# High and low halves in the sparse scores, and an order changed at four places of a two-block network kernel

## The chip, the core and the metric

The kernel runs on one core of a Trainium2 chip. The metric is the device time of one execution in microseconds (us), as the median of several runs. The core's engines work side by side and wait for each other by semaphores: TensorE (PE: matmuls into PSUM), VectorE (DVE), ScalarE (ACT), GpSimd (POOL) and SyncE (SP), which here issues DMAs. Each engine runs its own instructions strictly in order. Inputs, outputs and the state-space tables lie in HBM; everything between is in SBUF.

## The reference, cut to what matters

256 tokens of width 1024 pass two blocks of two layers each, in float32.

```python
# block 1: layer 0 short convolution, layer 1 dilated attention with partial rotary
h = h + mixer(rmsnorm(h)); h = h + relu(rmsnorm(h) @ up)**2 @ down          # mlp
h = h + sigmoid(rmsnorm(h) @ w_gate) * (p @ w_proj)                          # ple
# block 2, layer 0: h += ffn0; h += s5(rmsnorm(h)); h += ffn1; shared keys and values
# s5: per group of 16 channels 64 complex states, x_t = A x_{t-1} + B u_t, y = Re(C x)
y = gelu(y + d_skip * u); h = h + y * sigmoid(y @ w_glu)
# block 2, layer 1: h += ffn2; h += nsa(rmsnorm(h)); h += ffn3
qg = u @ w_qg                      # 16 heads of 64, and 48 gate columns
q = rmsnorm(qg[..., :1024]); gates = sigmoid(qg[..., 1024:])
o = gates[0] * o_cmp + gates[1] * o_selected + gates[2] * o_window
h = h + o @ w_o
# each branch: softmax(q @ k * scale + bias) @ v; 15 compressed keys, 256 selected, 256 window keys
```

## The kernel before, in words

All dense weights are one array of 280 units of 1 MB, 128 partitions by 2048 columns. They stream through a ring of three slots (`RING` = 3). For a unit SyncE loads `raw`, ScalarE copies it to `w_hi` (L1152, a rounded copy of it), VectorE subtracts `w_lo` (`split`, L1952), and TensorE multiplies. Activations are held transposed, channels on partitions, as `x_hi` and `x_lo` too, made in four pairs of chunks (`x_high` on ScalarE, `x_low` on VectorE). A slot comes free when TensorE is done with its unit, and only then can its next high half be written. A product in full accuracy is three matmuls (`exact`, L460 to L462):

```python
nc.tensor.matmul(out, a_hi, b_hi, start=start, stop=False, skip_group_check=True)
nc.tensor.matmul(out, a_hi, b_lo, start=False, stop=False, skip_group_check=True)
return nc.tensor.matmul(out, a_lo, b_hi, start=False, stop=stop, skip_group_check=True)
```

`double_unit` (L507, L509) does the same with two matmuls, of 512 and 256 columns. `zero` products (L481, L904) add zeros, and `keep_warm` issues them so that TensorE has work in a wait.

**Norms.** The scale of a norm isn't applied to the activations. ScalarE squares them (L1176), GpSimd adds the squares (`add_squares`, L1701), TensorE sums over partitions and later broadcasts (`norm_sum`, `norm_bcast`), VectorE and GpSimd make the inverse root, ScalarE copies it to `rs`. The stage is multiplied afterwards.

**Start and convolution.** VectorE begins with a chain of 31 operations on 128x32 (`link`, L2202 to L2221), from which ScalarE makes a sine and a cosine (L1363 and after). Then come low halves and the first splits. The convolution is four triples of units (`conv_triple` on each engine), then the residual stage `sc_out`, then `mlp0`, whose first norm is number `R_SC`. GpSimd does its norm R_IN, then `input_matrices`, which waits for the 31 operations and the sine and cosine, then `four_tables(0, R_SC)`:

```python
make_table(c)
if not c:
    norm(r)
make_table(c + 1)
```

A table is 1.8 MB, stored to HBM and loaded again in the state-space stage. ScalarE's squares are double-buffered, so its third square of a norm waits for GpSimd's first add of that norm (`sq_used`).

**Angles.** The rotary angles are eight small VectorE operations (`angles`, L2163 to L2182), one pair after each of the four gate steps of `ple0`.

**State-space stage.** After `ffn0`, `u5` = h x gain x norm scale is made in eight chunks, and VectorE, ScalarE and GpSimd move it to the layout of groups (`u2`). TensorE does eight `states` (each 24 products, L923) and eight `outputs` (L935, 16 products) and turns the result back (`turn_y`). Between the two VectorE turns the drive (L2405) and scans, GpSimd turns back. The gate unit `glu` follows.

**Sparse attention.** TensorE's queries are four units (`qg`), the gates 48 products of 48 columns between the first and the second unit. Per head `n_scores` multiplies query and keys in plain float32 (two products of 128 queries for the selected and window keys, one for 15 compressed keys per 128 queries). Softmax, transposes (`n_turn`) and values follow, three steps behind each other in a loop over heads. `out_part` multiplies two heads' output into the first two units of `w_o`; the third unit (L460) comes behind the loop, and behind it the fourth (`up_unit(g + 3, ...)`).

## Time and profile before

| | |
|---|---|
| median of 3 runs | 1919.35 us (1918.03 to 1920.93) |
| the profiled execution | 1921.98 us, its span 1920.1 us |
| granted TensorE clock, mean | 0.987 of full speed |
| chain that ended last | PE 84%, DVE 9%, ACT 4%, issue 2%, POOL 1% |
| L1952, weight splits on DVE | x277, 653.4 us, 2361 ns each |
| L1152, high halves of weights on ACT | x280, 534.1 us, 1909 ns each |
| HBM | 318.54 MB read, 174 GB/s over the span |

Times are microseconds from the start of the span; engines overlap, so busy shares don't add up. The chain that ended last is followed back from the last instruction. A line such as L460 is shared by all products that `exact` issues.

### The profile page before, as it was taken

Reading aid. Unit: us, or ns where it says so; the run is one execution under the profiler, and the core shown is the slowest. Engines: PE = TensorE matmul, PEld = TensorE weight load, DVE = VectorE, ACT = ScalarE, POOL = GpSimd, SP = SyncE. Lnnn points to the kernel's source line nnn. Section 1 sums busy time; section 2 is a strip of 40 time slices with the busy share of each in tenths; the row PEclk is TensorE's granted clock in tenths of the full one; section 3 lists DMA queues with packets and bytes.
Section 4 is the critical chain, followed back from the end, with each engine's and each line's share of the span. In section 5 each row is a group of like instructions: output and inputs, shape, how many; then the busy total and the mean of one; then the engine's idle time right before and its main releaser. Section 6 shows DMA issues by size and latency. Waiting matters only on the chain.

```text
span 1920.1 us, 31815 instructions
## 1 busy us (share of the span) xinstructions
PE 1860.1 (97%) x13410; PEld 1716.7 (89%) x13427; DVE 1284.7 (67%) x1503; ACT 927.2 (48%) x1214; POOL 635.5 (33%) x756
## 2 busy tenths in 40 slices
PE   8999999899999999999999989999999999999999
PEld 6979999899999899988997878998989989778998
DVE  6878666666664777677666756666656665657665
ACT  4354445444334554455444245444654454755443
POOL 6968880476753887010001620000000002420000
PEclk9999999999999999999999899999999998999999
DMA  6555564454444566557556315665355642015553
GB/s 243 187 186 214 214 215 181 151 187 165 155 165 144 172 216 215 209 194 289 193 181 214 116 73 205 220 219 182 137 169 193 211 179 88 23 39 181 189 184 110
DMA packets 54954, 336.35 MB, mean 175 GB/s; under 512 B 7915, under 2 KB 13084, under 8 KB 17948
## 3 DMA queue, kind: packets, MB, share of 16 engines
q1 hardware_dynamic: 45648, 297.51, 43.1%
q10 hardware_dynamic: 5068, 22.13, 3.0%
q0 software_dynamic: 4096, 14.68, 2.2%
q8 instruction: 106, 1.74, 0.4%
q14 instruction: 36, 0.29, 0.0%
HBM read 318.54 MB, written 15.75 MB: 174 GB/s over the span
## 4 chain that ended last, share of the span: by engine, by line
PE 84%; DVE 9%; ACT 4%; issue 2%; POOL 1%; ACTq 0%; DVEq 0%; POOLq 0%
PE psum L507 22%; PE psum L460 13%; PE psum L461 13%; PE psum L462 13%; PE psum L509 11%; DVE w_lo L1952 3%; ACT w_hi L1152 2%; DVE both L1959 1%; ACT both L1152 1%; PE psum L935 1%; PE psum L973 1%; PE psum L1093 1%; PE psum L1062 1%; DVE h L1965 1%; PE psum L923 1%
## 5 line engine op out<-in xcount | busy, mean ns | idle before, releaser
L1952 DVE TENSOR_TENSOR w_lo<-raw,w_hi 128x2048 fp32r<-128x2048 f32 x277 | 653.4, 2361 | 200.9 <-ACT w_hi L1152 198.1
L507 PE MATMUL psum<-both,w_hi 128*128 128x512 f32 x1984 | 702.7, 397 | 9.6 <-DVE both L1959 6.8
L1152 ACT ACTIVATE w_hi<-raw 128x2048 fp32r<-128x2048 f32 x280 | 534.1, 1909 | 179.7 <-PE psum L462 178.2
L509 PE MATMUL psum<-both,w_lo 128*128 128x256 f32 x1984 | 556.6, 281 | 0.0
L460 PE MATMUL psum<-both,w_hi 128*128 128x256 f32 x1600 | 464.2, 290 | 16.4 <-DVE both L1959 10.0
L507 PEld LDWEIGHTS psum<-both,w_hi 128*128 128x128 f32 x1984 | 372.7, 188 | 98.0 <-DVE both L1959 7.9
L461 PE MATMUL psum<-both,w_hi 128*128 128x256 f32 x1600 | 454.9, 284 | 0.0
L462 PE MATMUL psum<-both,w_lo 128*128 128x256 f32 x1600 | 454.8, 284 | 0.0
L509 PEld LDWEIGHTS psum<-both,w_lo 128*128 128x128 f32 x1984 | 375.5, 189 | 0.1
L460 PEld LDWEIGHTS psum<-both,w_hi 128*128 128x128 f32 x1600 | 308.6, 193 | 17.1 <-DVE both L1959 11.6
L461 PEld LDWEIGHTS psum<-both,w_hi 128*128 128x128 f32 x1600 | 308.8, 193 | 0.8 <-issue 0.2
L462 PEld LDWEIGHTS psum<-both,w_lo 128*128 128x128 f32 x1600 | 308.7, 193 | 0.0
L1701 POOL TENSOR_TENSOR ssum<-sq 128x512 f32<-128x512 f32 x11 | 18.5, 1683 | 735.9 <-ACT sq L1176 735.9
L1152 ACT ACTIVATE sq<-psum 128x512 f32<-128x512 f32 x120 | 71.7, 598 | 335.7 <-PE psum L509 334.6
L460 PE MATMUL psum<-hid_hi,w_hi 128*128 128x256 f32 x640 | 179.5, 280 | 0.3
L461 PE MATMUL psum<-hid_lo,w_hi 128*128 128x256 f32 x640 | 177.7, 278 | 0.0
L462 PE MATMUL psum<-hid_hi,w_lo 128*128 128x256 f32 x640 | 177.6, 277 | 0.0
L2048 DVE TENSOR_TENSOR ta<-psum,sq 128x512 f32<-128x512 f32 x76 | 52.3, 688 | 106.6 <-ACT sq L1152 106.4
L460 PEld LDWEIGHTS psum<-hid_hi,w_hi 128*128 128x128 f32 x640 | 120.2, 188 | 3.2 <-issue 1.6
L462 PEld LDWEIGHTS psum<-hid_hi,w_lo 128*128 128x128 f32 x640 | 120.8, 189 | 0.0
L461 PEld LDWEIGHTS psum<-hid_lo,w_hi 128*128 128x128 f32 x640 | 120.2, 188 | 0.1
L2099 DVE TENSOR_TENSOR tc<-psum,sq 128x512 f32<-128x512 f32 x44 | 30.4, 692 | 64.3 <-ACT sq L1152 64.3
(402 smaller groups left out, 2504.4 us busy)
## 6 DMA issues: line engine op xcount, KB each, us to landing
raw<-in_weights SPq DMA_DIRECT2D x280, 1024.0 KB, 4.8
table<-tables ACTq DMA_DIRECT2D x8, 1792.0 KB, 8.5
tables<-st POOLq DMA_DIRECT2D x16, 512.0 KB, 4.3
tables<-st POOLq DMA_DIRECT2D x8, 256.0 KB, 5.8
tables<-turns POOLq DMA_DIRECT2D x8, 256.0 KB, 4.4
w<-in_cmp_w ACTq DMA_DIRECT2D x4, 512.0 KB, 5.2
tbl<-in_cmp_w ACTq DMA_DIRECT2D x4, 512.0 KB, 5.2
tbl<-bias_v SPq DMA_DIRECT2D x128, 16.0 KB, 4.7
```

What stands on the lines that cost most here:

```text
L460: nc.tensor.matmul(out, a_hi, b_hi, start=start, stop=False, skip_group_check=True)
L461: nc.tensor.matmul(out, a_hi, b_lo, start=False, stop=False, skip_group_check=True)
L462: return nc.tensor.matmul(out, a_lo, b_hi, start=False, stop=stop, skip_group_check=True)
L507: nc.tensor.matmul(bank, wh[:, cols], both[x][:, c].rearrange("p e t -> p (e t)"), start=c == 0, stop=False, skip_group_check=True)
L509: return nc.tensor.matmul(bank[:, 0:SEQ], wl[:, cols], x_hi[x][:, c], start=False, stop=c == KC - 1, skip_group_check=True)
L923: last = nc.tensor.matmul(SB_[c % 4][:, at:at + SK], w_[:, jj, ri], u2[:, jj, c, :], start=True, stop=True, skip_group_check=True)
L935: last = nc.tensor.matmul(y_of(c, jj), x5[c % 2][:, ri, jj, 0:SK], q_[:, jj, ri], start=False, stop=ri == 1, skip_group_check=True)
L973: last = nc.tensor.matmul(DB[half][0:2 * NCMP, 0:P], blk[rows, l, :, :].rearrange("p c n -> p (c n)"), [w1, w1v][kind][rows, l, :], start= ...
L1152: copy = lambda out, in_, **kw: nc.scalar.activation(out, in_, ACT.Copy, **kw)
L1952: tt(w_lo[:, g % RING], raw[:, g % RING], w_hi[:, g % RING].bitcast(F32), ALU.subtract).then_inc(sem["lo_ready"], 1)
L2048: tt(ta[:], hi_part(pair), low[into], ALU.add).then_inc(sem["a_sum"], 1)
L2099: tt(tc[:], hi_part(B_PAIR), low[1], ALU.add).then_inc(sem["b_sum"], 1)
```

## The change

- Start: VectorE's 31 operations go behind the first (13 of them) and the second triple (18) of the convolution, ScalarE's sine and cosine behind its second. ScalarE's squares R_IN come between its copies of the first weights. SyncE issues the load of the constants behind the second weight unit. GpSimd's code is the same.
- Angles: the third and fourth pair are issued behind the last low half of `ple0`.
- State space: gains are applied without the norm's scale ahead of the norm; the scale is multiplied into `u2`, chunk by chunk, afterwards, from a copy of 32-token rows that ScalarE makes. `states` waits for one chunk's multiply. 14 and 5 + 5 zero products are added, 24 and others taken out. One weight split moves from the end of `ffn0` to behind the scans. The order of the norm's parts changes.
- Sparse attention: gates are 24 products with 48 weight columns and 256 moving ones, copied, transposed and then put through the sigmoid. Scores are three products each of halves; ScalarE and VectorE make the halves of the keys and the queries. The compressed keys are padded to 16 columns.
- The third unit of `w_o` moves piecewise into the end of the loop over heads (`third_rows`).

The diff, cut to its core and moved to the left:

```diff
@@ -274,7 +274,10 @@
-    q2 = sb("q2", [P, NQ, SEQ], scope=t)
+    ks_hi = sb("ks_hi", [P, 2, 2, SEQ], F32R, scope=t)
+    ks_lo = sb("ks_lo", [P, 2, 2, SEQ], F32R, scope=t)
...
@@ -418,7 +422,9 @@
     sp.dma_start(raw[:, u], A["weights"][u]).then_inc(raw_landed[u], 16)
     if u == 0:
         sp.wait_ge(sem["h_landed"], 16 * PAIRS)
+    if u == 1:
         sp.dma_start(con[:], A["con"]).then_inc(sem["con_landed"], 16)
+        sp.wait_ge(raw_landed[1], 16)
...
@@ -903,18 +909,16 @@
 keep_warm(20, XB)
 norm_sum(R_FFN0)
+clear_sums()
+keep_warm(4, XB)
+norm_bcast(R_FFN0)
 keep_warm(6, XB)
-norm_bcast(R_FFN0)
-keep_warm(24, XB)
-clear_sums()
 def states(c):
...
-    for name in ("u2_dve", "u2_act", "u2_pool"):
-        pe.wait_ge(sem[name], c // 4 + 1)
+    pe.wait_ge(sem["u2_dve"], 2 + c + 1)
...
@@ -942,9 +946,16 @@
+def add_zeros(n, bank):
+    for _ in range(n):
+        nc.tensor.matmul(bank, zero[:, 0:P], zero[:], start=False, stop=False, skip_group_check=True)
 for c in range(3):
     states(c)
+add_zeros(14, DB[0])
 for c in range(KC):
+    if c >= KC - 2:
+        add_zeros(5, DB[3])
...
@@ -1028,13 +1039,18 @@
 n, g, x = R_FFN2, BASE["qg"], XBUF[R_FFN2]
 up_unit(g, 0, x, q_bank[0], (sem["xl_ready"], XBASE[n], 1), lambda: norm_sum(n))
 pe.wait_ge(sem["wg_lo_ready"], 1)
-for t in range(TT):
-    for c in range(KC):
-        last = exact(DB[0][:, t * 64:t * 64 + 3 * NH],
-                     tuple(xx[x][:, c, t * P:(t + 1) * P] for xx in (x_hi, x_lo)),
-                     (wg_hi[:, c, :], wg_lo[:, c, :]), c == 0, c == KC - 1)
+for c in range(KC):
+    last = exact(DB[0][0:3 * NH, 0:SEQ], (wg_hi[:, c, :], wg_lo[:, c, :]), (x_hi[x][:, c], x_lo[x][:, c]),
+                 c == 0, c == KC - 1)
 last.then_inc(sem["gate_done"], 1)
 norm_bcast(n)
+def turn_gates():
+    pe.wait_ge(sem["gate_sig"], 1)
+    for t in range(TT):
+        last = nc.tensor.transpose(DB[1][:, t * 64:t * 64 + 3 * NH], gate_rows[:, t * P:(t + 1) * P],
+                                   ident[0:3 * NH, 0:3 * NH])
+    last.then_inc(sem["gate_done"], 1)
...
@@ -1052,19 +1068,18 @@
     if hd:
         pe.wait_ge(sem["n_log"], hd)
-    pe.wait_ge(sem["k_sq"], 3 + 2 * (hd // 4) + 2)
-    b, a, rows = hd % 2, hd // 8, slice((hd % 2) * HD, (hd % 2 + 1) * HD)
-    q = q2[rows, hd // 2]
-    for br in range(2):
-        bank = DB[br]
-        nc.tensor.matmul(bank[:, 0:P], q[:, 0:P], ks[rows, br, a, 0:P], start=True, stop=True,
-                         skip_group_check=True)
...
+    pe.wait_ge(sem["n_lo"], 1 + hd // 4)
+    if not hd:
+        pe.wait_ge(sem["wg_lo_ready"], 2)
+    a, rows = hd // 8, slice((hd % 2) * HD, (hd % 2 + 1) * HD)
+    q = [(x_hi[0][rows, hd // 2, t * P:(t + 1) * P], x_lo[0][rows, hd // 2, t * P:(t + 1) * P])
+         for t in range(TT)]
+    keys = tuple(k[rows, :, a, :] for k in (ks_hi, ks_lo))
+    exact(DB[0][:, 0:2 * P].rearrange("p (r k) -> p r k", r=2), q[0], tuple(k[:, :, 0:P] for k in keys), True, True)
+    exact(two(DB[1]), q[1], keys, True, True)
     for t in range(TT):
-        last = nc.tensor.matmul(DB[0][:, 3 * P + t * NCMP:3 * P + (t + 1) * NCMP],
...
+        last = exact(DB[0][:, 2 * P + t * (NCMP + 1):2 * P + (t + 1) * (NCMP + 1)], q[t],
+                     (kc_hi[rows, a, :], kc_lo[rows, a, :]), True, True)
     last.then_inc(sem["n_s"], 1)
...
@@ -1109,8 +1126,22 @@
         if ch == KC - 1:
             last.then_inc(sem["unit_done"], 1)
-up_unit(g_q + 1, 0, x, q_bank[1], mid=lambda: q_sums(0))
-pe.wait_ge(sem["gate_sig"], 1)
+def third_rows(c0, c1):
+    if c0 == 0:
+        pe.wait_ge(sem["lo_ready"], g + 3)
+        pe.wait_ge(sem["n_log"], NH)
+        nc.tensor.matmul(DB[0], zero[:, 0:P], zero[:], start=True, stop=False, skip_group_check=True)
+    pe.wait_ge(sem["n_lo"], 4 + c1)
+    for c in range(c0, c1):
+        for q in range(2):
+            last = exact(DB[0][:, q * SEQ:(q + 1) * SEQ], wide(slot(g + 2), c, q),
+                         (x_hi[0][:, c], x_lo[0][:, c]), False, c == KC - 1)
+    if c1 == KC:
+        last.then_inc(sem["unit_done"], 1)
+up_unit(g_q + 1, 0, x, q_bank[1], mid=lambda: (turn_gates(), q_sums(0)))
+pe.wait_ge(sem["gate_sig"], 2)
...
@@ -1126,6 +1157,8 @@
+    if step >= NH - 1:
+        third_rows(*((0, 2), (2, 4), (4, 5))[step - NH + 1])
...
@@ -1133,16 +1166,9 @@
     if 1 <= step <= NH:
         n_turn(step - 1)
 out_part(KC - 2)
-pe.wait_ge(sem["lo_ready"], g + 3)
-pe.wait_ge(sem["n_log"], NH)
-nc.tensor.matmul(DB[0], zero[:, 0:P], zero[:], start=True, stop=False, skip_group_check=True)
-for c in range(KC):
-    if c == 2:
-        out_part(KC - 1)
...
+third_rows(5, 7)
+out_part(KC - 1)
+third_rows(7, 8)
 up_unit(g + 3, 0, 0, DB[1])
...
@@ -1321,7 +1347,8 @@
     if r != R_FFN3:
         for m in range(PAIRS):
             residual(r, m, x)
-    split(g + 3 * FFN_PAIRS - 1)
+    if f:
+        split(g + 3 * FFN_PAIRS - 1)
...
@@ -1352,18 +1379,11 @@
 copy(w_hi[:, 0], raw[:, 0]).then_inc(sem["hi_ready"], 1)
 for m in range(1, PAIRS):
     x_high(R_IN, m)
-for m in range(PAIRS):
-    squares(R_IN, m)
 for g in range(1, RING):
+    squares(R_IN, 2 * g - 2)
+    squares(R_IN, 2 * g - 1)
     act.wait_ge(raw_landed[g], 16)
     copy(w_hi[:, g], raw[:, g]).then_inc(sem["hi_ready"], 1)
-act.wait_ge(sem["sm_dve"], S5_R)
...
@@ -1376,7 +1396,15 @@
 norm(R_IN)
 conv_triple(0, 0, 0)
-for k in range(0, PAIRS - 1):
+conv_triple(3, 0, 1)
+act.wait_ge(sem["sm_dve"], S5_R)
+act_fn(sm[:, 8], sm[:, 5], ACT.Abs).then_inc(sem["sm_act"], 1)
+act_fn(e_one[:, :, 1], sm[:, 5], ACT.Sin).then_inc(sem["sm_act"], 1)
+act.wait_ge(sem["sm_act"], 3)
+act.wait_ge(sem["fill_done"], 4)
+act_fn(e_one[:, :, 0], sm[:, 8], ACT.Sin, scale=-1.0, bias=halfpi[:]).then_inc(sem["sm_act"], 1)
+for k in range(1, PAIRS - 1):
     conv_triple(3, k, k + 1)
 residual_stage("sc_out", R_SC)
...
@@ -1516,6 +1543,12 @@
 move(0)
 move(1)
+act.wait_ge(sem["bcast_ready"], R_FFN0 + 1)
+steps = norm_bank(R_FFN0)[:, SEQ:2 * SEQ].rearrange("p (k i) -> p i k", i=SL)
+for i in range(SL):
+    last = copy(rs[32 * i:32 * i + 32, 0, 0:SK], steps[32 * i:32 * i + 32, i])
+last.then_inc(sem["rs_ready"], 1)
+split(BASE["glu"] - 1)
 act.wait_ge(sem["u2_dve"], 2)
 act.wait_ge(sem["u2_pool"], 2)
...
@@ -1606,11 +1639,15 @@
 g = BASE["qg"]
 act.wait_ge(sem["wg_landed"], 16)
 copy(wg_hi[:], wg[:]).then_inc(sem["wg_hi_ready"], 1)
+act.wait_ge(sem["k_ready"], 3)
+copy(ks_hi[:], ks[:])
...
+copy(kc_hi[:, :, 0:NCMP], kcmp[:]).then_inc(sem["wg_hi_ready"], 1)
 norm(R_FFN2)
...
-    act_fn(q2[:, 2 * u:2 * u + 2].rearrange("p c t -> p (c t)"), q_bank[u], ACT.Copy,
+    act_fn(x_hi[0][:, 2 * u:2 * u + 2], two(q_bank[u]), ACT.Copy,
            scale=col("qn")).then_inc(sem["k_sq"], 1)
     if u >= 2:
...
@@ -1618,10 +1655,12 @@
            ACT.Square).then_inc(sem["k_sq"], 1)
 q_copy(0)
+act.wait_ge(sem["gate_done"], 1)
+copy(gate_rows, DB[0][0:3 * NH, 0:SEQ]).then_inc(sem["gate_sig"], 1)
 split(g)
-act.wait_ge(sem["gate_done"], 1)
+act.wait_ge(sem["gate_done"], 2)
 for t in range(TT):
-    last = act_fn(gate[:, t], DB[0][:, t * 64:t * 64 + 3 * NH], ACT.Sigmoid, scale=rs_tok[:, t:t + 1])
+    last = act_fn(gate[:, t], DB[1][:, t * 64:t * 64 + 3 * NH], ACT.Sigmoid, scale=rs_tok[:, t:t + 1])
...
@@ -2192,44 +2232,22 @@
         gated(PAIRS * l + m + 1, two([XB, DB[0], DB[1], DB[2]][m]), m)
         if m < PAIRS - 1:
             split(g + 1 + m)
-        if l == 0:
+        if l == 0 and m < 2:
             angles(m)
     x_low(r, PAIRS - 1)
+    if l == 0:
+        angles(2)
+        angles(3)
     split(g + PAIRS)
-dve.wait_ge(sem["sm_act"], 1)
-link(tt(sm[:, 1], are, sm[:, 0], ALU.mult))
-link(ts(sm[:, 1], sm[:, 1], 2.0 ** -S5_HALVINGS, None, ALU.mult))
...
-for m in range(2):
-    x_low(R_IN, m)
+x_low(R_IN, 0)
 first_split(0)
-for m in range(2, PAIRS):
+for m in range(1, PAIRS):
     x_low(R_IN, m)
 for g in range(1, RING):
     first_split(g)
...
@@ -2273,7 +2291,30 @@
     split(g0 + 2, k)
 conv_triple(0, 0, 0)
-for k in range(0, PAIRS - 1):
+dve.wait_ge(sem["sm_act"], 1)
+link(tt(sm[:, 1], are, sm[:, 0], ALU.mult))
+link(ts(sm[:, 1], sm[:, 1], 2.0 ** -S5_HALVINGS, None, ALU.mult))
+    link(tt(sm[:, 2], sm[:, 2], sm[:, 1], ALU.mult))
...
+conv_triple(3, 0, 1)
+for _ in range(S5_HALVINGS):
+    link(stt(sm[:, 2], sm[:, 2], 2.0, sm[:, 2], ALU.add, ALU.mult))
...
+link(dve.reciprocal(sm[:, 12], sm[:, 11]))
+assert count[0] == S5_R
+for k in range(1, PAIRS - 1):
     conv_triple(3, k, k + 1)
 residual_stage("sc_out", R_SC)
...
@@ -2371,21 +2412,35 @@
 ffn(0, R_FIN, R_FFN0, x=False)
-norm(R_FFN0)
-dve.wait_ge(sem["rs_ready"], R_FFN0 + 1)
 def by_step(ap):
     return ap.rearrange("p (k i) -> p i k", i=SL)
+def gains(half):
+    for c in range(4 * half, 4 * half + 4):
+        ts(u5[:, c].rearrange("p (i k) -> p i k", i=SL), by_step(h[:, c]), col("s5mix", c), None,
+           ALU.mult).then_inc(sem["u5_ready"], 1)
+def move(half):
+    dve.wait_ge(sem["u5_ready"], 4 * half + 4)
+    for i, q in [(0, q) for q in range(JJ)] + [(1, 0), (1, 1)]:
+        last = dve.tensor_copy(u2[32 * i:32 * i + 32, q, 4 * half:4 * half + 4, :],
+                               u5_of(q, half)[:, :, i, :])
+    last.then_inc(sem["u2_dve"], 1)
+dve.wait_ge(sem["h_ready"], hbase(R_FFN0) + PAIRS)
+gains(0)
+move(0)
+gains(1)
+norm(R_FFN0)
+move(1)
+dve.wait_ge(sem["rs_ready"], R_FFN0 + 1)
 for c in range(KC):
-    stt(u5[:, c].rearrange("p (i k) -> p i k", i=SL), by_step(h[:, c]), col("s5mix", c), by_step(rs[:, 0]),
-        ALU.mult, ALU.mult).then_inc(sem["u5_ready"], 1)
-    if c % 4 == 3:
-        half = c // 4
-        dve.wait_ge(sem["u5_ready"], c + 1)
...
-        last.then_inc(sem["u2_dve"], 1)
+    if c % 4 == 0:
+        dve.wait_ge(sem["u2_dve"], 2)
+        dve.wait_ge(sem["u2_act"], c // 4 + 1)
+        dve.wait_ge(sem["u2_pool"], c // 4 + 1)
+    tt(u2[:, :, c, :], u2[:, :, c, :], rs[:, 0, 0:SK].unsqueeze(1).broadcast_to([P, JJ, SK]),
+       ALU.mult).then_inc(sem["u2_dve"], 1)
 def gelu_low(b):
...
@@ -2420,6 +2475,7 @@
     for ri in range(2):
         dve.tensor_tensor_scan(z5[c % 2][:, ri], decay, a_[:, ri], 0.0, ALU.mult,
                                ALU.add).then_inc(sem["z_ready"], 1)
+split(BASE["glu"] - 1)
 for b in range(4):
     gelu_low(b)
 for m in range(PAIRS):
...
@@ -2505,6 +2561,18 @@
 tt(wg_lo[:], wg[:], wg_hi[:].bitcast(F32), ALU.subtract).then_inc(sem["wg_lo_ready"], 1)
 norm(R_FFN2)
 ts(qe[:], var_tok[:], EPS / NSCALE ** 2, None, ALU.mult).then_inc(sem["q_var"], 1)
+dve.wait_ge(sem["wg_hi_ready"], 2)
+tt(ks_lo[:], ks[:], ks_hi[:].bitcast(F32), ALU.subtract)
...
+tt(kc_lo[:, :, 0:NCMP], kcmp[:], kc_hi[:, :, 0:NCMP].bitcast(F32), ALU.subtract).then_inc(sem["wg_lo_ready"], 1)
+def query_low(u):
+    cs = slice(2 * u, 2 * u + 2)
+    dve.wait_ge(sem["k_sq"], 3 + 2 * u + 2)
+    stt(x_lo[0][:, cs], two(q_bank[u]), col("qn"), x_hi[0][:, cs].bitcast(F32), ALU.mult, ALU.subtract)\
+        .then_inc(sem["n_lo"], 1)
+query_low(0)
 def query_sums(u):
     dve.wait_ge(sem["q_var"], 1)
```

## Rows read from the trace of the kernel before

**Rows 1.** Page part 1: busy time, share and instructions of each engine.

```profile
PE 1860.1 (97%) x13410; PEld 1716.7 (89%) x13427; DVE 1284.7 (67%) x1503; ACT 927.2 (48%) x1214; POOL 635.5 (33%) x756
```

**Rows 2.** Stretch, us; busy of PE, PEld, DVE, ACT, POOL; clock; DMA share; GB/s.

```profile
1069.50:1083.20 13.70, 12.41 (x56) 11.74 (x56) 8.30 (x13) 0.00 (x0) 9.81 (x9) 0.50 0.37 135
1083.20:1103.00 19.80, 19.80 (x166) 18.26 (x166) 15.39 (x22) 5.47 (x7) 14.62 (x15) 1.00 0.50 187
1588.35:1602.00 13.65, 13.65 (x64) 13.47 (x63) 0.92 (x3) 4.23 (x6) 0.00 (x0) 0.50 0.16 66
1641.00:1699.00 58.00, 57.12 (x366) 44.41 (x367) 39.01 (x124) 36.60 (x167) 23.62 (x43) 1.00 0.05 19
```

**Rows 3.** VectorE's time line, first and last of 31 (start, us, operation, [wait before]).

```profile
7.32 0.19 DVE L2202 TENSOR_TENSOR sm<-vec,sm 128x32 f32<-128x32 f32 x1 [7.32 <-ACT sm L1348]
...
13.99 0.35 DVE L2221 RECIPROCAL sm<-sm 128x32 f32<-128x32 f32 x1
```

**Rows 4.** Time line of TensorE, its first product.

```profile
18.31 0.61 PE L481 MATMUL psum<-zero 128*128 128x512 bf16 x1 [7.34 <-DVE w_lo L2227]
```

**Rows 5.** Time line of ScalarE, start.

```profile
10.45 1.89 ACT L1152 ACTIVATE w_hi<-raw 128x2048 fp32r<-128x2048 f32 x1
...
24.30 1.28 ACT L1363 ACT_TABLE_LOAD   x1
```

**Rows 6.** Time line of VectorE, first and last split of a triple.

```profile
86.63 2.29 DVE L1952 TENSOR_TENSOR w_lo<-raw,w_hi 128x2048 fp32r<-128x2048 f32 x1 [0.91 <-PE psum L462]
...
98.89 2.48 DVE L1952 TENSOR_TENSOR w_lo<-raw,w_hi 128x2048 fp32r<-128x2048 f32 x1 [1.11 <-ACT w_hi L1152]
```

**Rows 7.** Time line of GpSimd: input matrices, their slowest operation, last store, first add.

```profile
28.23 0.25 POOL L1735 TENSOR_TENSOR a<-mag,e_one 128x32 f32<-128x32 f32 x1
...
33.26 2.36 POOL L1754 TENSOR_TENSOR sm<-sm 128x32 f32<-128x32 f32 x1
...
107.04 0.54 POOL L1833 DMA_DIRECT2D tables<-st  x1
...
111.35 1.39 POOL L1701 TENSOR_TENSOR ssum<-sq 128x512 f32<-128x512 f32 x1 [3.76 <-ACT sq L1176]
```

**Rows 8.** Stretch of the table, L1952 alone: us, DVE busy, clock, DMA, GB/s.

```profile
28.20:107.70 79.50, 30.68 (x13) 1.00 0.52 186
```

**Rows 9.** Time line of VectorE, the split of the second unit of mlp0.

```profile
123.24 4.49 DVE L1952 TENSOR_TENSOR w_lo<-raw,w_hi 128x2048 fp32r<-128x2048 f32 x2 [1.44 <-ACT w_hi L1152]
```

**Rows 10.** Time line of VectorE, third pair of angles.

```profile
346.55 1.48 DVE L2176 SCALAR_TENSOR_TENSOR ang<-ang 128x256 f32<-128x256 f32 x1
```

**Rows 11.** Time line of TensorE, first product of qkv.

```profile
350.06 0.58 PE L460 MATMUL psum<-both,w_hi 128*128 128x256 f32 x1 [4.91 <-DVE both L1959]
```

**Rows 12.** Time line of VectorE at the state-space stage.

```profile
1047.07 2.55 DVE L1952 TENSOR_TENSOR w_lo<-raw,w_hi 128x2048 fp32r<-128x2048 f32 x1 [3.95 <-ACT w_hi L1152]
...
1062.07 0.69 DVE L2405 TENSOR_TENSOR ta<-psum,table 128x512 f32<-128x512 f32 x1
```

**Rows 13.** Time line of TensorE: first output, first product of glu.

```profile
1070.79 3.67 PE L935 MATMUL psum<-table,con 128*64 128x128 f32 x16 [4.21 <-POOL con L1912]
...
1115.27 0.47 PE L460 MATMUL psum<-both,w_hi 128*128 128x256 f32 x1
```

**Rows 14.** Time line of TensorE: gate products, and the next unit.

```profile
1587.24 0.29 PE L460 MATMUL psum<-wg_hi,both 128*128 128x48 f32 x1 [0.37 <-DVE wg_lo L2505]
...
1588.16 0.27 PE L462 MATMUL psum<-wg_hi,both 128*128 128x48 f32 x1
...
1597.16 0.78 PE L460 MATMUL psum<-both,w_hi 128*128 128x256 f32 x1
```

**Rows 15.** Time line of TensorE: a head's first scores, and what follows them.

```profile
1688.35 0.49 PE L1060 MATMUL psum<-ks,q 64*128 64x128 f32 x2
...
1690.20 0.64 PE L1091 MATMUL psum<-ptc,vcmp 15*64 15x256 f32 x2
```

**Rows 16.** Time line of TensorE, end of the loop over heads.

```profile
1700.94 0.64 PE L1091 MATMUL psum<-ptc,vcmp 15*64 15x256 f32 x2 [1.25 <-ACT ptc L1152]
```

More of the change, by code:

```diff
@@ L1087, in n_values @@
                 if b == 0 and ch >= 2:
[L1088 removed]
+                    pe.wait_ge(sem["n_lo"], 4 + ch - 1)
+                if ch < 2:
+                    pe.wait_ge(sem["n_lo"], 4)
                 pe.wait_ge(sem["n_ta"], hd + 1)
@@ L1135, in _ @@
             out_part(KC - 2)
-            pe.wait_ge(sem["lo_ready"], g + 3)
-            pe.wait_ge(sem["n_log"], NH)
-            nc.tensor.matmul(DB[0], zero[:, 0:P], zero[:], start=True, stop=False, skip_group_check=True)
-            for c in range(KC):
-                if c == 2:
-                    out_part(KC - 1)
-                for q in range(2):
-                    last = exact(DB[0][:, q * SEQ:(q + 1) * SEQ], wide(slot(g + 2), c, q),
-                                 (x_hi[0][:, c], x_lo[0][:, c]), False, c == KC - 1)
-            last.then_inc(sem["unit_done"], 1)
+            third_rows(5, 7)
+            out_part(KC - 1)
+            third_rows(7, 8)
             up_unit(g + 3, 0, 0, DB[1])
@@ L1608, in _ @@
             copy(wg_hi[:], wg[:]).then_inc(sem["wg_hi_ready"], 1)
+            act.wait_ge(sem["k_ready"], 3)
+            copy(ks_hi[:], ks[:])
+            copy(kc_hi[:, :, NCMP:], kcmp[:, :, 0:1])
+            copy(kc_hi[:, :, 0:NCMP], kcmp[:]).then_inc(sem["wg_hi_ready"], 1)
             norm(R_FFN2)
@@ L2153, in ffn @@
                 last_sums(g + 3 * FFN_PAIRS - 1, r, 0.5, x)
-                split(g + 3 * FFN_PAIRS - 1)
+                if f:
+                    split(g + 3 * FFN_PAIRS - 1)
             def gated(count, other, m):
```

67 lines of the change are left out of this document (27 added, 40 removed).

## The prediction

> **What bounds the kernel now.** I read the busy totals of the page first, then the stretches with granted clock, then the time line of one engine at a time around each edited place. TensorE is busy 1860.1 of 1920.1 us [rows 1], so an edit pays only if it removes TensorE work, an idle gap of TensorE, or a stretch at the lower of its two clock levels. In a full-clock stretch it starts a product every 19.80/166 = 0.119 us; in the two long half-clock stretches, 13.70 and 13.65 us, the step is 0.213 us and more [rows 2]. Both lie at edited places, the state-space stage and the query gates. Four places are edited: start, angles, state-space stage, sparse attention.
>
> **Start, what it gives.** VectorE now does 31 small operations from 7.32 to 14.34, 7.0 us or 0.226 us each [rows 3], before it touches the first activations; TensorE sits idle for 7.34 us and starts at 18.31 [rows 4]. ScalarE had the first high half done at 12.34 [rows 5]. After the change VectorE splits the first unit right then: 12.34 + 2.3 = 14.65, 3.7 us earlier. The squares hold the norm, so unit 1 starts about 2.9 us earlier (23.6 for 26.5, an estimate). The later constant load is needed only near 24 us and lands in time.
>
> **Start, what it costs.** The 31 operations come back behind the first and the second triple of the convolution, and GpSimd's input matrices wait for all of them. A triple costs VectorE 14.7 us (86.63 to 101.37 [rows 6]). The first would end at 45.2 (49.1 less 2.9, less 1 because GpSimd is not in the way); 13 operations bring 48.1, the second triple 63.3, 18 operations 67.4. ScalarE, which stands waiting there, adds the table load of 1.28 us [rows 5] and four small operations: 69.6. Behind its wait stand the copy and both high halves of the third triple, so TensorE's unit 9 waits until about 74.3 where it would have been free at 70.4; with two small waits behind it the conv stage is then some 3 us later than before, not 3 earlier.
>
> GpSimd begins the input matrices at 69.6 in place of 28.23 [rows 7]. Its code is otherwise unchanged: input matrices, then the whole first table, and only then the adds of squares for the next norm. It ended this work at 107.6 and the first add came at 111.35 [rows 7], so the slack is 3.8 us and the work comes 41 us later. The work took 79.4 us, in which VectorE spent 30.7 us in 13 weight splits [rows 8]; a GpSimd operation of 128x32, otherwise 0.25 us, lasted 2.36 us beside one of them [rows 7]. I take the splits as full stops: 79.4 - 30.7 = 48.7 us of own work. From 69.6 on VectorE can do only 8 splits before the chip stalls (18.9 us), so the table ends at 69.6 + 48.7 + 18.9 = 137.2. Bounds: no stop at all, 118.3; every stop as before, 149.0. I am nearest to the middle since the count of splits is in the code.
>
> Who waits: the third square of ScalarE needs the first add, and behind it on ScalarE stand the last high half of the activations and the high halves of the next weights. From the end of the table: add 1.4, square 0.6, high half 0.9, square 0.6, w_hi 1.9, so VectorE's split starts 5.5 us after it, at 142.7; before it started at 123.24 [rows 9]. That is +19.4 us. TensorE has then been idle for some 17 us and restarts at the lower clock; an average of 5 us of dense work at half speed is 2.5, less the 0.7 that a later wait hides: +1.9. Start in all: **+21** (bounds +1 and +33).
>
> **Angles.** The fourth gate step waits for the third pair of angle steps, 346.55 to 348.5 [rows 10]; TensorE's gap of 4.91 us before 350.06 [rows 11] ends on the low half that comes right behind it. With that pair moved, the gap ends 2.0 us sooner, and the last low half comes another 0.7 us sooner for the fourth pair. The moved pairs (2.7 us) now lie behind the last low half and before a split that TensorE needs a unit later, which hides them. **-2.7** (0 to -4).
>
> **State-space stage.** One weight split leaves the front: the split of 1047.07 lasted until 1049.6 and held the mean of the norm [rows 12], 1 us. The gains (4 x 0.4 us) and the first moves run before the norm instead of behind it; only the second moves and 8 products of 128x256 (0.35 us apart) stay behind it. By hand: scale ready 1051.9, GpSimd's second moves 1053.3, first states at 1052.8, all eight scaled at 1055.6. VectorE's first turn, at 1062.07 before [rows 12], comes at 1055.6. The first output, 1070.79 [rows 13], follows the first drive by GpSimd's 5 us and three states and 14 added zero products (3.0 us): 1064.6. From there before took 44.5 us to the first gate product at 1115.27 [rows 13], 13.70 us of it at the lower clock [rows 2]. With TensorE busy from 1052.8 on I expect no such stretch: 8 outputs of 1.92 (16 steps of 0.12), 5 states of 2.93 (24 and a wait), 3 turns of 0.6 and 10 zeros of 0.21 are 34 us, to which GpSimd's last step, held up by the split moved right behind the last scan, adds 2.3: 1101. The gates start 14 us sooner; one is taken off for the table loads, which come a few us closer to their use. **-13** (-6 if the low clock stays, -15).
>
> **Sparse attention, gates.** 48 products of 48 columns from 1587.24 to 1596.5 become 24 of 256 columns: 24 x 0.119 = 2.9 us in place of 9.3. The next unit, which began at 1597.16 [rows 14], was at half clock until 1602.0 [rows 2], 22 products that lose 2.0 us. Two small turns add 0.35, and the copy they wait for is done before the middle of the unit. Sum -8.1, with 0.5 for the norm sum behind it -8.6. The activity that held the clock down is gone, but the short gaps ahead of it stay: a third of a chance that it falls anyway, at 2.5 us.
>
> **Scores.** A head's scores take 1690.20 - 1688.35 = 1.85 us [rows 15]. After: three products of 256 columns at 0.119, three of 512 at 0.235 (twice the step), six of 16 columns. For a 48-column product the rows show 0.115 us (1587.24 to 1588.16, eight steps [rows 14]), and I price the 16-column ones so: 0.36 + 0.71 + 0.69 = 1.76 us, 0.09 less a head: **-1.4**. TensorE is busy 57.12 of 58 us there [rows 2], so this is path. The low halves on VectorE (4 x 0.7) and of the keys (1.2) lie in its waits for TensorE.
>
> The Trainium skill, TensorE: Matmul & The Clock Gate, "Wait — 56ns, not 53.3ns?", gives small products a start-to-start floor of about 25 ns. By that the six 16-column products of a head would take 0.15 us and not 0.69, and the scores would give another 9 us. The page's section "LDWEIGHTS (loading the stationary operand)" has 107 ns for 128 columns of weights, and by that, the trace agrees.
>
> **Projection rows.** 30 products move into three gaps of which the first is 1.25 us before 1700.94 [rows 16]. They fill them, but the path is another: the unit behind needs a ring slot that the first projection unit frees, and its high half can't start until the last head is in; then it takes 1.9 + 2.3 us. Before, 4.3 us of rows covered that; now 0.7 us do. So the gap moves to the end, 3.3 us wide, and I expect the clock to fall behind it: **+1.7** (0 to +3, or -3.5 if the split were not last).
>
> **Sum.** 21.3 - 2.7 - 13 - 8.6 + 0.9 - 1.4 + 1.7 = -1.8; the terms are good to several us each, and I take -2. The profiled execution took 1921.98 us, 1.9 beyond its span and 2.6 above the median 1919.35; against that median the forecast is 1917.
>
> **Rivals.**
> (a) GpSimd gains nothing from VectorE's stall, because its stops are not the splits. For it: its operations in the table are longer than their shortest everywhere. Against: the 2.36 us operation. It ends at 149.0 in place of 137.2, 12 us more: 1929. This is the case on the other side; it decides from an end of the table 6 us later than forecast.
> (b) The clock falls in the state-space stage all the same, since its products are as small as before. For it: before, three stretches of such products did not bring the clock back. Against: 20 us of them at 1083 to 1103 kept it [rows 2]. Gain 6 in place of 13: 1924.
> (c) GpSimd is hardly stopped once TensorE and ScalarE wait, and its own work is shorter than 48.7: end at 128, 9 us less: 1908.
> (d) The late table costs nothing, the norm's adds not being behind it in effect: 21 less and 3 of the early start more: 1893. Against: the add came 3.8 us behind the table in program order.
> (e) The 16-column products are cheaper than the 48-column row: at 0.03 us each a head saves another 0.5 us, 8 to 9 in all: 1908. Nothing in the trace is narrower and quicker; the skill's floor above would give it.
>
> **Chances.** Forecast 0.50 (its own range 1911 to 1923), (a) 0.17, (b) 0.11, (c) 0.12, (d) 0.05, (e) 0.05. I leave (d) and the end of (a) outside: 1906 to 1928. A change under 0.2%, 3.8 us, can't be told from none. Of the forecast half lies within that, four tenths below and a tenth above: faster 0.50 x 0.4 + 0.12 + 0.05 + 0.05 = 0.42; slower 0.05 + 0.17 + 0.06 = 0.28; same 0.30.
>
> **What would show it.** On GpSimd the input matrices begin near 70 and the first add of the second norm near 137; TensorE has a gap of 15 us or more between 120 and 145, and mlp0 starts 21 us late. The first turn of the state space comes 6 us nearer to the end of ffn0, the half-clock stretch behind it is gone, and glu starts 13 us nearer. The gates take 3 us. A gap near 3 us stands before the last projection unit. If GpSimd's start is not late, or mlp0 is not, the forecast's main term is wrong and the time is below 1905.

## The result, and the profile after

| | before | after |
|---|---|---|
| median | 1919.28 us (1918.03 to 1920.93) | 1930.91 us (1929.1 to 1934.91), 4 runs each |
| ratio | | 1.0063, 95% interval 1.0047 to 1.0078 |
| profiled execution, its span | 1921.98, 1920.1 us | 1929.1, 1927.3 us |
| granted clock, mean | 0.987 | 0.986 |

The change makes the kernel slower by 0.6%. The forecast was 1917, so it had the sign and the size wrong. The profiled execution after is the fastest of its four, that of before is 1 us slower than the slowest of its other runs; span to span the loss is 7.2 us, median to median 11.6. The page of after, part 1:

```profile
PE 1856.1 (96%) x13409; PEld 1709.3 (89%) x13409; DVE 1297.6 (67%) x1518; ACT 930.4 (48%) x1220; POOL 626.4 (32%) x756
```

TensorE's busy time fell by 4.0 us against [rows 1] while the span grew by 7.2, so its idle time grew by 11. To see where, I set the 280 weight splits of the two traces side by side; they come in the same order in both but for one. How much later a split starts in after than in before is then a running account:

| place | after less before, us | step | forecast |
|---|---|---|---|
| split of mlp0's second unit (123.2 before) | +17.0 | | |
| end of mlp0 | +19.4 | +19.4 | +21.3 |
| qkv | +17.6 | -1.8 | -2.7 |
| end of ffn0 | +17.8 | +0.2 | |
| glu | +13.8 | -4.0 | -13 |
| ffn1 to the query units | +15.8 | +2.0 | |
| behind the gates | +7.6 | -8.2 | -7.7 |
| end of the sparse stage | +6.8 | -0.8 | +0.3 |
| end | +7.2 | +0.4 | |

Two steps of this table lie mostly in the clock. Behind the angles the kernel before had 6.8 us at half clock (from 349.3), after has none there. In ffn1 before had 3.4 us (from 1148.0) and after has 6.8 (from 1161.5), which is most of the +2.0.

**Start.** Time line of GpSimd, then of TensorE (an entry is start, us, line, operation, and in brackets the idle time before it and what ended it). The first input matrix comes at 68.09 (28.23 in [rows 7]), the table's last store at 134.59, and the first add of the norm right behind it; TensorE is idle for 6.57 us before 103.59 and for 12.68 before 140.18.

```profile
68.09 0.26 POOL L1774 TENSOR_TENSOR a<-mag,e_one 128x32 f32<-128x32 f32 x1 [42.65 <-issue]
...
135.15 1.27 POOL L1740 TENSOR_TENSOR ssum<-sq 128x512 f32<-128x512 f32 x1
```

```profile
140.18 0.80 PE L513 MATMUL psum<-both,w_hi 128*128 128x512 f32 x1 [12.68 <-DVE both L1998]
```

**State space.** Two stretches of after: the eight chunks, and the half clock at the last output (columns as in [rows 2]).

```profile
1073.10:1110.10 37.00, 36.37 (x291) 32.10 (x292) 34.58 (x50) 5.09 (x6) 27.83 (x26) 1.00 0.41 150
1120.70:1131.00 10.30, 7.95 (x36) 7.39 (x37) 1.27 (x2) 3.60 (x4) 1.47 (x2) 0.51 0.08 32
```

The half-clock stretch that stood behind the first output is gone. One at the last output has grown: 10.2 us from 1120.5, where the kernel before had 3.4 from 1110.5. In the first row both TensorE and VectorE are full. The last output, time line of TensorE, before and after:

```profile
1110.43 3.63 PE L935 MATMUL psum<-table,con 128*64 128x128 f32 x16 [2.85 <-POOL con L1912]
```

```profile
1122.36 3.67 PE L939 MATMUL psum<-table,con 128*64 128x128 f32 x16 [4.09 <-POOL con L1951]
```

The last chunk on VectorE, and the split that follows it (L2462, left out, is as L2461):

```profile
1109.83 0.66 DVE L2460 TENSOR_TENSOR sq<-psum,table 128x512 f32<-128x512 f32 x1
1110.41 0.41 DVE L2461 TENSOR_TENSOR sq<-psum,table 128x256 f32<-128x256 f32 x1
...
1111.25 1.24 DVE L2469 TENSOR_TENSOR sq<-sq 128x512 f32<-128x512 f32 x1
1112.63 2.52 DVE L2476 TENSOR_TENSOR_SCAN ssum<-table,sq 128x256 f32<-128x256 f32 x2
1115.07 2.26 DVE L1991 TENSOR_TENSOR w_lo<-raw,w_hi 128x2048 fp32r<-128x2048 f32 x1
```

A chunk takes 1115.07 - 1109.83 = 5.24 us. GpSimd's last step, beside the split and the gelu's low halves, takes 7.1 us (4.8 in the kernel before, 1105.61 to 1110.38), and TensorE's last output waits 4.08 us for it:

```profile
1115.23 3.25 POOL L1943 TENSOR_TENSOR con<-ssum,table 128x512 f32<-128x512 f32 x1 [0.63 <-DVE ssum L2476]
...
1120.88 1.44 POOL L1951 TENSOR_TENSOR con<-con,n 128x512 f32<-128x512 f32 x1
```

**Sparse stage.** Time line of TensorE in after: first gate product and a later one, the first and two of the last products of a head's scores, what follows them, and the last projection unit, with its gap.

```profile
1603.07 0.32 PE L466 MATMUL psum<-both,wg_hi 128*48 128x256 f32 x1 [0.37 <-DVE wg_lo L2561]
...
1695.14 0.39 PE L466 MATMUL psum<-ks_hi,both 64*128 64x256 f32 x1
...
1696.44 0.25 PE L468 MATMUL psum<-kc_hi,both 64*128 64x16 f32 x1
1696.56 0.25 PE L466 MATMUL psum<-kc_hi,both 64*128 64x16 f32 x1
...
1696.96 0.64 PE L1108 MATMUL psum<-ptc,vcmp 15*64 15x256 f32 x2
...
1728.48 0.58 PE L466 MATMUL psum<-both,w_hi 128*128 128x256 f32 x1 [2.90 <-DVE w_lo L1991]
```

The gates' last product starts at 1605.85, so they take 2.9 us. A head's scores take 1.82 us against 1.85 in [rows 15], and a 16-column product starts 0.12 us after the one before.

### The profile page after: what moved, and what is told of

The parts are those of the page before. It is cut to its first block and busy times, and to the rows that moved or that the text cites. A ratio compares the mean times of both kernels' runs of the same rounds, so it can differ in the third digit from the quotient of the medians.

```text
span 1927.3 us, 31816 instructions
## 1 busy us (share of the span) xinstructions
PE 1856.1 (96%) x13409; PEld 1709.3 (89%) x13409; DVE 1297.6 (67%) x1518; ACT 930.4 (48%) x1220; POOL 626.4 (32%) x756
## 5 line engine op out<-in xcount | busy, mean ns | idle before, releaser
L1998 DVE SCALAR_TENSOR_TENSOR both<-h,vec,both 128x256 fp32r<-128x256 f32 x88 | 53.1, 650 | 36.8 <-ACT both L1178 36.7
```

Source lines behind the costliest of these rows:

```text
L1998: last = stt(x_lo[XBUF[r]][:, c], h[:, c], gain(r, c), x_hi[XBUF[r]][:, c].bitcast(F32), ALU.mult, ALU.subtract)
```

## The experiments

Ratios are against runs of the kernel before on the same chip, whose median was 1919.6 to 1921.0 in each group. "The changed kernel" is the one of 1930.91. Differences in us between kernels are of medians, some of them from two chips, so about 1 us of each is not told apart from the chips.

### The start

**Chain at the front.** VectorE's and ScalarE's blocks go back to their old places; squares and constants stay changed.

```diff
+            dve.wait_ge(sem["sm_act"], 1)
+            link(tt(sm[:, 1], are, sm[:, 0], ALU.mult))
...
             x_low(R_IN, 0)
```

> The changed kernel with VectorE's 31 operations back at the front and the sines behind ScalarE's first weights; all else stays changed. Theory (GpSimd's late start of the input matrices holds back the norm of mlp0, 19.2 us): GpSimd starts near 28, TensorE's 12.7 us gap in front of mlp0's second unit and most of the 6.6 us gap before it are gone, the half-clock stretch of 130 to 148 too; 1930.9 - 19 = 1912, between 1909 and 1914. Rival (the order of the squares and the later load of the constants carry part of the loss): the gap at 97 us stays and the time is 1916 to 1920.

1909.42 us, ratio 0.9943 (0.9928 to 0.9957). 21.5 us came back. The input matrices begin at 27.75 and both gaps are back at 1.24 and 1.28 us. The rival on squares and constants is out.

**The start alone,** on the kernel before (VectorE's, ScalarE's and SyncE's start edits and no other).

> The kernel before, with the changed start alone. Theory (late chain, late input matrices, late norm): 19.2 us as the traces stand to each other, 21.3 by the forecast, so 1938.5 to 1941.5. Rival (part of it is taken back later by waits that were there anyway): below 1937.

1939.17 us, ratio 1.0103 (1.0089 to 1.0117): +19.6. The loss stands alone as well.

**The norm ahead of the table.** Inside `four_tables` the call of the norm goes, too.

```diff
-            four_tables(0, R_SC)
+            norm(R_SC)
+            four_tables(0, None)
```

> The changed kernel with the late chain, but GpSimd does the norm of mlp0 right behind the input matrices and before the first table. Theory (the table stands between GpSimd's late start and the norm): the gap of 12.7 us before mlp0's second unit shrinks to about 1, but the table work, some 36 us, now comes after it, ends near 320 in place of 297, and the norm behind mlp0, due near 303, waits for it some 15 us: 1926 to 1935, the gap only moved. Rival (ScalarE's and VectorE's own late work makes the gap): the gap before mlp0's second unit stays above 8 us, and the second comes on top: above 1940.

1944.27 us (1937.27 to 1948.11), ratio 1.012 (1.0094 to 1.0146): the rival's time, but not its cause. The gap before mlp0's second unit is gone, as expected, but the table's lateness didn't wait for the next norm: TensorE itself has products of the table (L608) in its program during mlp0, and it stands there for GpSimd. Time line of TensorE in this kernel:

```profile
159.68 1.97 PE L608 MATMUL psum<-con,ab 128*128 128x128 f32 x8 [14.15 <-POOL st L1857]
```

Another 5.57 us of that kind follow at 202.6. So the table is needed through two engines, and putting the norm ahead of it on GpSimd doesn't hide its late start.

**Spread chain.** 9 operations behind the second first split, 10 in the wait for the norm, 12 behind it, the sines in the first triple; and the late split of the next section.

```diff
             first_split(1)
+            dve.wait_ge(sem["sm_act"], 1)
...
             first_split(2)
             norm(R_IN)
+            for n in (3, 2):
...
```

> The changed kernel with VectorE's 31 operations spread over its idle times in the first 35 us (9 behind the second first split, 10 in the wait for the norm, 12 behind it), the sines in the first triple, and the state-space split behind the gelu's low halves. Theory: GpSimd begins the input matrices near 35, the table ends near 112, the early start of 3 us is kept and the late table costs nothing; with the 6 to 7 us of the later split: 1909.4 - 3 - 6 = 1900 to 1903. Rival (a table that ends past 108 already holds the norm up us by us): 1904 to 1908.

1908.65 us, ratio 0.9941 (0.9924 to 0.9957). No better than the chain at the front with the split unmended, and just above the rival's range. The input matrices began at 35.3, the first add of the norm came at 114.18 (111.35 in [rows 7]), and TensorE has gaps of 2.63 us at 60 and 2.06 at 98.6, with half clock from 352 to 362; qkv began 3.5 us late. The rival's cause isn't shown: against the kernel before, the splits are 1.6 us early at 45, already 2.5 late at 71, and still 2.8 late at mlp0's second unit, so the loss arose in the convolution, ahead of that norm. Why the gap at 60 came stays open.

### The state-space stage

**The stage as before, and the stage alone.** In the first, the stage's edits are undone in the changed kernel; in the second they are the only edits to the kernel before.

> The changed kernel with the state-space stage (norm order, gains, moves, waits, zeros, the split) as it was before; all else stays changed. Theory (the stage's change gives only 2 to 4 us, as the two traces stand to each other, since VectorE and GpSimd set the pace): 1930.9 + 2 to 4 = 1933 to 1935. Rival (the stage gave the 13 us of the forecast and another place took them): 1942 to 1945.

> The kernel before, with the changed state-space stage alone. Theory (VectorE and GpSimd set the pace): 4 to 5 us faster, as its undoing cost 4.9: 1914.5 to 1916. Forecast's step: 13 faster, 1906. Rival (gains of one place are eaten by the clock in the next): 1917 to 1919.

1935.78 us, ratio 1.0081 (1.0065 to 1.0096): the stage gives 4.9 us there, a little more than expected. Alone 1918.14, ratio 0.9992 (0.9983 to 1.0001): 1.5 us by medians, 3.5 by the splits around the stage. That is the rival's range and not the theory's, but the two traces don't show its cause: they differ by 3.5 at the stage and still by 3.0 at the end, as do the two profiled executions. Both are far from 13.

**GpSimd relieved.**

```diff
-                tt(n2_[:, 0], z[:, 1], e[:, 2], ALU.mult)
+                tt(n2_[:, 0, :, 0:2], z[:, 1, :, 0:2], e[:, 2, :, 0:2], ALU.mult)
...
-                tt(x, x, n2_, ALU.add).then_inc(sem["x_ready"], 1)
+                tt(x[:, :, :, 0:2], x[:, :, :, 0:2], n2_[:, :, :, 0:2], ALU.add).then_inc(sem["x_ready"], 1)
```

GpSimd leaves out most of the second products and of the sum (2 of 16 columns are done), so only the pace of this kernel is read.

> The changed kernel, where GpSimd's turn of the states is left out but for its first product (the two second products and the sum work on 2 of 16 columns). What is read is the pace of the state-space stage. Theory (VectorE and GpSimd stop each other): VectorE's scans take 1.27 us a pair in place of 2.52 and its sum 0.69 in place of 1.24, a chunk comes every 4.9 us as TensorE allows in place of 5.24, the first output is 3 us and the last about 8 us sooner: 1921 to 1924. Rival (VectorE's scans are slow of themselves once TensorE and ScalarE are busy): the chunk stays at 5.2 us and only GpSimd's own last step is saved, 4 us: 1925 to 1928.

1920.95 us, ratio 0.9998 (0.9989 to 1.0008): 10 us less than the changed kernel, at the lower edge of the expectation. VectorE's time line, the same chunk:

```profile
1108.82 0.69 DVE L2460 TENSOR_TENSOR sq<-psum,table 128x512 f32<-128x512 f32 x1 [1.14 <-issue]
...
1110.28 0.69 DVE L2469 TENSOR_TENSOR sq<-sq 128x512 f32<-128x512 f32 x1
1111.10 1.27 DVE L2476 TENSOR_TENSOR_SCAN ssum<-table,sq 128x256 f32<-128x256 f32 x2
```

The scan pair takes 1.27 in place of 2.52 us and the sum 0.69 in place of 1.24, though nothing of VectorE's was changed: 1.8 us a chunk is GpSimd's doing. The products that read PSUM are as long as before. Not all of it reached the path. Counted from the end of ffn0, the first output came no sooner (3 us were expected) and VectorE's last chunk began only 1.2 us sooner, since TensorE's own chunk takes 4.9 us there. The last scan ended 3.0 us sooner, GpSimd's last step took 4.8 us in place of 7.1, and the half clock was gone, 2.2 us: glu began 7.5 us sooner. Part of that is GpSimd's work left out, so it isn't the price of the stops alone.

The Trainium skill, SBUF — State Buffer, "Who interferes with whom", has it that a VectorE instruction with two SBUF inputs contends with a GpSimd instruction that reads SBUF, and that one with at most one SBUF input, outside the 2-port modes, does not; by the page's "Summary: rules for kernel authors" the second to issue is blocked until the first finishes. The trace agrees on who contends: the sum and the scans stretch, the products out of PSUM (0.66, 0.41, 0.41 us) don't.

**Late split,** and **GpSimd's last step alone.** The second adds the marked line to the first.

```diff
-            split(BASE["glu"] - 1)
+            dve.wait_ge(sem["x_ready"], KC)    # the second alone
             for b in range(4):
                 gelu_low(b)
+            split(BASE["glu"] - 1)
```

> The changed kernel with the weight split behind the last scan moved behind the four low halves of the gelu. Theory (the last GpSimd step is slowed by VectorE work beside it, 7.1 us in place of 4.6): the split's 2.3 us go, the three low halves stay beside it, so GpSimd ends about 1.5 us sooner, the gap of TensorE shrinks from 4.1 to about 2.5, and the clock still falls: 1928.5 to 1930. Rival (the split alone is what stops GpSimd): the gap shrinks to 1.5 or less, the clock stays, and the stage is 5 us shorter: 1925 to 1926.

> As the one before, and the low halves of the gelu wait until GpSimd's last step is done, so VectorE does nothing beside it. Theory (VectorE's operations and GpSimd's stop each other): GpSimd's last step takes 4.0 to 4.6 us instead of 7.1, TensorE's gap is 1 to 1.6 us, the clock does not fall there, glu begins 5 us sooner relative to the end of ffn0: 1924 to 1927. Rival (GpSimd's last step is slow of itself): 7 us remain and the time is 1929 to 1932.

1923.86 us, ratio 1.002 (1.001 to 1.0029), and 1925.04, ratio 1.002 (1.001 to 1.003). GpSimd's last step in the first, then in the second:

```profile
1116.68 1.63 POOL L1943 TENSOR_TENSOR con<-ssum,table 128x512 f32<-128x512 f32 x1 [0.63 <-DVE ssum L2476]
...
1120.28 1.18 POOL L1951 TENSOR_TENSOR con<-con,n 128x512 f32<-128x512 f32 x1
```

```profile
1117.19 1.27 POOL L1943 TENSOR_TENSOR con<-ssum,table 128x512 f32<-128x512 f32 x1 [0.63 <-DVE ssum L2476]
...
1119.98 1.18 POOL L1951 TENSOR_TENSOR con<-con,n 128x512 f32<-128x512 f32 x1
```

4.8 us and 4.0 in place of 7.1, gaps of TensorE 1.77 and 0.97 in place of 4.08, and no half clock behind either. For the first, my theory gave the split too little: it alone brought 7 us, the rival's case and a little more. By the splits around the stage it brought 5.8. The second came out as expected, GpSimd's step at 4.0 us, but the low halves brought 0.8 us more at the stage and nothing that the time shows. One split of 2.3 us, put where nothing waited for it, cost 7.

**Without the added zeros.** The spread kernel without its 24 zero products.

```diff
-            add_zeros(14, DB[0])
...
-                    add_zeros(5, DB[3])
```

> As the one before, without the 24 added zero products of the state-space stage. Theory (they only fill waits for GpSimd and keep the clock): a gap of 3 to 4 us stands before the first output, the half-clock stretch behind it is back as in the kernel before, and the time is 5 to 7 us above the one before, 1906 to 1909. Rival (they are in the way of the first outputs): 1 to 3 us faster than it. Third: no difference within 1 us, the clock stays by itself.

1908.17 us, ratio 0.9935 (0.992 to 0.9949), against 1908.65: the third case. Half-clock stretches came at 1099 and 1140, and one at 1707 went.

### The smaller terms

**Both mends,** and on it **rows back** and **angles back**.

> The changed kernel with the chain back at the front (as in the first experiment, 1909.4) and the state-space split behind the gelu's low halves (7.0 off the changed kernel by itself). Theory (the two losses are apart and add up): 1909.4 - 6 to 7 = 1902.5 to 1904. Rival (the clock takes the later split's gain back when the stage starts earlier): 1907 to 1910.

1903.22 us (1903.03 to 1903.39), ratio 0.9909 (0.9896 to 0.9922): the best full kernel here, 17 us below the kernel before on its chip. The two losses add up.

```diff
-                    third_rows(*((0, 2), (2, 4), (4, 5))[step - NH + 1])
...
-            third_rows(5, 7)
+            third_rows(0, 2)
             out_part(KC - 1)
-            third_rows(7, 8)
+            third_rows(2, 8)
```

> As the one before, with the third unit of the output projection back behind the loop over heads. By the forecast's step (the moved rows only shift a gap to the end and let the clock fall, +1.7): 1.7 us faster than the one before. Rival (the rows fill three gaps of 1.3 us and cost nothing after): 1 to 3 us slower. From the two traces, where scores and rows together moved by -0.4 us: within 1 us.

> The kernel with the chain at the front, the late split and the rows back behind the loop, timed once more beside the one before, on the same chip: 1903.65 before, so 1903 to 1904.5.

1903.65 and 1903.93, ratios 0.9911 (0.9898 to 0.9924) and 0.9914 (0.9899 to 0.9929): no difference, where the forecast's step had 1.7 us. The moved rows exchange three gaps of 1.3 us for one of 2.90, with 6.8 us of half clock beside it that the kernel with the rows back doesn't have.

```diff
-                    if l == 0 and m < 2:
+                    if l == 0:
                         angles(m)
```

> As two before, with the third and fourth pair of angle steps back behind the third and fourth gate step. Theory: 2.7 us slower (forecast's step) or, by the drift between the two traces, 1.8. Rival (the split or low halves of the next unit wait in their place): within 0.5 us.

1906.06 us (1904.6 to 1913.94), ratio 0.9936 (0.9921 to 0.995): 2.8 slower, the forecast's size. The two traces don't bear the forecast's way to it. With the pairs moved, TensorE's gap on the third low half goes from 4.91 us to 3.34, but the next, on the last low half, grows from 0.34 to 1.50, since the half clock from 348.9 to 352.3 that follows the long gap is gone and TensorE is there sooner. TensorE's first product of the last low half then comes 1.65 us sooner, counted from the splits ahead of it. But a third gap appears in the kernel with the moved pairs, 0.87 us before 357.53, where TensorE waits for VectorE's part of the norm, behind the pairs and a split. So 0.5 us is left at the split behind it (361), the rival's case by the trace. The rest of the 2.8 came far from the edit, at half-clock stretches from 823.4 (1.5 us) and 1137.4 (1.3 us), which the kernel with both mends doesn't have.

**Gates alone,** on the kernel before.

> The kernel before, with the gates alone as 24 products of 256 columns and two turns. Theory (9.3 us of products become 2.9 and the half-clock stretch behind goes): 1919.3 - 8 = 1910 to 1912. Rival (the clock falls in any case behind the short gaps ahead of the gates): 1913 to 1915.

1913.79 us, ratio 0.9965 (0.9953 to 0.9977): 6.7 by the medians, 8.3 by the splits of its trace at the gates. The time is in the rival's range, but the clock didn't fall at the gates; half clock came at 824, where before has none.

**Fewer 16-column products,** which leaves out four of a head's six and makes the compressed scores less exact, and **scores and rows as before**, both on the kernel with both mends.

```diff
-                                 (kc_hi[rows, a, :], kc_lo[rows, a, :]), True, True)
+                                            kc_hi[rows, a, :], start=True, stop=True, skip_group_check=True)
```

> The changed kernel with the chain at the front and the late split (1903.2), where a head's compressed scores are left at their first product each (high half by high half): four of six products of 16 columns a head left out, 64 in all, so the compressed scores are less exact. Theory (such a product costs 0.115 us on the path, as the trace shows, and the clock falls behind them near 1605 in most traces): 64 x 0.115 = 7.4 us, and up to 2.7 more if that half-clock stretch goes: 1893 to 1896. Rival (they cost 0.025 to 0.03 us each): 1.6 to 2 us, 1901 to 1902.

1895.47 us, ratio 0.9878 (0.9865 to 0.9892): 7.75 us for 64 products. That is 0.121 us each, but the half-clock stretch at 1605 went too. Between two splits of the loop over heads, at full clock in both traces (1618.6 to 1699.8 and 1616.0 to 1692.2), 44 products fewer made 5.05 us, 0.115 each. A product of 16 columns costs nearly what one of 256 does (0.119). That closes the forecast's rival (e), and by the Trainium skill's section "LDWEIGHTS (loading the stationary operand)" of TensorE: Matmul & The Clock Gate, named in the prediction there with 107 ns, the trace agrees.

> The changed kernel with the chain at the front, the late split, and the scores and the third projection unit as they were before: plain float32 scores, rows behind the loop. It differs from the next only in the scores. Forecast's step (the split scores save 0.09 us a head): 1.4 slower than the next, 1905. Theory (they save 0.03 us a head, 0.5 us, but the clock falls behind their 16-column products near 1605 in 8 of 11 traces, 2.7 us): 2 us faster than the next, 1901 to 1902.

1904.16 us (1902.24 to 1905.23), ratio 0.9917 (0.9903 to 0.9931), against 1903.93 of its twin with the split scores: no difference. Here my theory fell, and the forecast's step of 1.4 us isn't seen either. The half-clock stretch near 1605 is absent without the split scores, but others stand elsewhere (348.6 to 358.8, 1137 to 1144), and the time comes out the same.

## Why the prediction was wrong

**Start: right.** Forecast +21.3; +19.4 in the traces, +21.5 undone, +19.6 alone. The steps held one by one: input matrices at 68.09 (69.6), table end 135.15 (137.2), split of the second unit at 140.2 (142.7). The forecast's 5 us of work at half speed behind the gap came from no row; the half clock lasted 7.7 us there (140.2 to 147.9) and cost 2.4 us for the 1.9. In between VectorE did 8 splits, as counted, in 21.1 us for 18.9:

```profile
68.00:135.20 67.20, 21.07 (x8) 0.89 0.37 134
```

Rival (a), by which GpSimd gains nothing, gave 1929, close to the measured time, but by accident: the table ended where the forecast had it, and its sign of an end 6 us later didn't come.

**State space: this step failed,** -13 forecast, -1.5 to -4.9 measured. "8 outputs of 1.92 (16 steps of 0.12), 5 states of 2.93 (24 and a wait), 3 turns of 0.6 and 10 zeros of 0.21 are 34 us" sums TensorE's work and so assumes that TensorE waits only for the 2.3 us added behind it. On before's time line (the times of after less 17.8) the first output came at 1067.3 for 1064.6, glu at 1109.9 for 1101. Of these 9 us, 2.6 are VectorE's gains and moves, which stand ahead of the norm's mean: 1055.4 for 1052.8 at the first states. The other 6.2 lie behind the first output. TensorE waited 0.88 and 4.08 us before its last two outputs where the sum had 2.3, and the half clock made the last output 3.67 us long instead of 1.96 and the turn behind it 1.11 instead of 0.66. That is 4.8; the last 1.4 us I have not traced to a wait.

GpSimd's last step had the forecast's length, 4.8 us in before and 2.3 for the split, 7.1. What was left out is that TensorE had stood waiting there before the change: 1.45 and 2.85 us before its last two outputs, and half clock with the last. The last chunk, which no other work of TensorE covers, takes VectorE 5.24 us instead of the 3.5 without GpSimd beside it, and GpSimd then 7.1 instead of 4.0. I had taken splits as full stops of GpSimd in the table, and priced TensorE without its waits in the stage where both other engines work at every chunk. The late split tests it: with that alone mended, the stage's 4.9 us and the mend's 7.0 are 12 of the 13 (4.0 and 5.8 by the splits around the stage). Rival (b) had the clock fall, and it did, at another place; that the longer gap made the stretch longer is argued from the two kernels with the late split, which have none there.

**Gates, scores, rows: right in size.** -8.2 and -6.7 for -7.7; 1.82 us a head for 1.76; rows and scores together 0 for +0.3.

**Angles: luck.** -2.8 for -2.7 by the medians, but only 0.5 us of it stands at the edit. The last low half came 1.65 us sooner instead of 2.7, and the moved pairs were not hidden: VectorE did them ahead of the norm's next step, for 0.87 us of waiting. The -1.8 in the table is mostly the half clock that before had at 349 and after had not: the kernel with the gates alone, without an edit there and with 3.4 us of it instead of 6.8, was 1.3 us sooner behind it.

**What stays open.** The single terms (start +21.5 or +19.6, state space -4.9 or -1.5, angles -2.8, gates -6.7, the rest 0) add to between 5 and 10.5 us, the medians say 11.6 and the spans 7.2. The clock is large enough for that. In the kernel with the changed start alone the state-space stage is as before, and yet it took 4.7 us less in its trace, with 6.8 us of half clock behind the first output instead of 13.7; its +19.6 holds such a gain. In the four executions of the changed kernel the granted clock was 0.986, 0.986, 0.985 and 0.981 at 1929.1, 1931.6, 1930.2 and 1934.9 us, and in the traces half-clock stretches come and go at 368, 1605 and 1156 with no edit near them. I take the difference for that; no run here shows it.

## What to carry to other kernels

When a stage is rearranged so that TensorE no longer waits, sum up the other engines' time per step too, with the durations that they have when they run at once, and treat the last step by itself: nothing covers it. Work that "can run any time" on VectorE is not free beside a GpSimd operation on the path. And before a chain is moved off an engine that waits, follow its results through every engine: here 7 us of VectorE work, moved out of the way, let GpSimd start 40 us later and everything behind it 19.
